# Six pairs of token-mixer projections as seven block products each, with operand sums on GpSimd

## What is computed

```python
h = rmsnorm(x, norm_mix) * (1.0 + sc1) + sh1            # sc, sh, g: 6 modulation rows, silu(cond) @ w_ada
proj = h @ w_in                                          # 1024 -> 7 groups of 512 columns
xr, gr, q_raw, ff, fb, iv, og = split(proj)
y_lru = rmsnorm(h_f + h_b, norm_lru) * gelu(gr)          # two RG-LRU scans over xr
y_hg  = hgrn2(q_raw, ff, fb, iv, og, ...)                # 4 heads, forward and backward, states 128x128
x = x + g1 * (concat([y_lru, y_hg]) @ w_out)
h = rmsnorm(x, norm_ffn) * (1.0 + sc2) + sh2
x = x + g2 * expert_choice_ffn(h, ...)                   # 16 SwiGLU experts, capacity 2T/16
y = rmsnorm(x, norm_final)
```

## Time and profile before

| | us |
|---|---|
| median of 3 runs (lowest, highest) | 958.57 (958.35, 960.14) |
| the profiled execution | 958.34 |
| its span, first to last instruction | 956.6 |
| PE busy | 928.8 (97%) |
| VectorE busy | 516.9 (54%) |
| ScalarE busy | 289.7 (30%) |
| GpSimd busy | 101.2 (11%) |

### The profile page before, as it was taken

How to read it: one execution, slowest core, us unless ns; L and a number is a source line. 1 busy time by engine, 2 the same in 40 slices (tenths; PEclk the granted TensorE clock), 3 DMA queues, 4 the chain that set the end, 5 groups by cost and what they waited for, 6 DMA issues and landing times.

```text
span 956.6 us, 19027 instructions
## 1 busy us (share of the span) xinstructions
PE 928.8 (97%) x8298; PEld 423.3 (44%) x8298; DVE 516.9 (54%) x1269; ACT 289.7 (30%) x507; POOL 101.2 (11%) x115
## 2 busy tenths in 40 slices
PE   5999999999999999999999999999999999999996
PEld 4555756768667554463222222222222223333332
DVE  4487667663654743764464461752636516444096
ACT  5137756564653824323020100200202002010103
POOL 3200010000000022112102002011020110100100
PEclk9999999999999999999999999999999999999999
DMA  9991014404029443168999999999999999999993
GB/s 333 334 386 52 2 55 157 160 5 176 10 92 367 174 164 150 66 240 323 403 399 404 408 416 408 415 401 413 418 405 413 405 413 425 401 426 413 412 380 122
DMA packets 52930, 276.15 MB, mean 289 GB/s; under 512 B 4400, under 2 KB 12752, under 8 KB 39920
## 3 DMA queue, kind: packets, MB, share of 16 engines
q1 hardware_dynamic: 45744, 253.77, 66.1%
q0 software_dynamic: 5584, 15.89, 5.7%
q10 hardware_dynamic: 1520, 5.28, 1.4%
HBM read 261.91 MB, written 13.01 MB: 287 GB/s over the span
## 4 chain that ended last, share of the span: by engine, by line
PE 79%; DMA 8%; DVE 5%; ACT 3%; issue 3%; POOL 0%; SPq 0%; POOLq 0%; DVEq 0%; ACTq 0%
PE pa L699 44%; PE p L699 34%; DMA ring<-in_w_up_dram 3%; DMA reg_e<-in_w_up_dram 3%; DMA ring<-in_w_ada_dram 1%; ACT reg_c L1374 1%; ACT L1374 1%; ACT reg_d L1374 1%; DMA reg_c<-h_rows,row_s 0%; ACT reg_b L1374 0%; DVE reg_a L2246 0%; DVE reg_b L1867 0%; PE p L854 0%; DVE reg_a L2241 0%; DVE reg_b L1838 0%
## 5 line engine op out<-in xcount | busy, mean ns | idle before, releaser
L699 PE MATMUL pa<-ring,reg_b 128*32 128x512 f32 (+1 forms) x1696 | 250.0, 593 | 0.7 <-DMA ring<-in_w_up_dram 0.5
L699 PE MATMUL p<-ring,reg_b 128*16 128x512 f32 (+1 forms) x1920 | 215.3, 592 | 1.1 <-issue 1.1
L699 PE MATMUL pa<-reg_a,ring 128*128 128x512 f32 (+1 forms) x640 | 191.2, 453 | 2.2 <-DVE reg_a L1730 1.5
L699 PEld LDWEIGHTS pa<-ring,reg_b 128*32 128x32 f32 (+1 forms) x1696 | 82.5, 117 | 143.7 <-issue 142.6
L699 PEld LDWEIGHTS pa<-reg_a,ring 128*128 128x128 f32 x640 | 98.3, 191 | 80.1 <-issue 79.9
L699 PEld LDWEIGHTS p<-ring,reg_b 128*16 128x16 f32 (+1 forms) x1920 | 63.9, 102 | 143.9 <-issue 143.9
L2142 DVE STREAM_TRANSPOSE reg_b<-reg_b 32x128 f32<-32x128 f32 x384 | 116.3, 303 | 5.9
L2158 DVE TENSOR_TENSOR reg_b<-reg_b,pa 128x512 f32<-128x512 f32 x16 | 11.0, 686 | 146.7 <-PE pa L699 146.4
L1374 ACT ACTIVATE reg_b<-pa 128x512 f32<-128x512 f32 (+1 forms) x20 | 12.4, 619 | 239.8 <-PE pa L699 239.8
L1374 ACT ACTIVATE reg_b<-reg_d,x_mod 128x128 f32<-128x128 f32 (+1 forms) x112 | 39.4, 440 | 140.7 <-PE p L699 140.7
L1374 ACT ACT_TABLE_LOAD x57 | 73.1, 1283 | 4.6 <-issue 2.8
(11 more groups left out here) (335 smaller groups left out, 937.4 us busy)
## 6 DMA issues: line engine op xcount, KB each, us to landing
ring<-in_w_gate_dram SPq DMA_DIRECT2D x25, 2048.0 KB, 21.1
ring<-in_w_down_dram SPq DMA_DIRECT2D x24, 2048.0 KB, 24.1
ring<-in_w_up_dram SPq DMA_DIRECT2D x22, 2048.0 KB, 21.5
ring<-in_w_ada_dram SPq DMA_DIRECT2D x8, 2048.0 KB, 8.5
ring<-in_w_in_dram SPq DMA_DIRECT2D x6, 2048.0 KB, 19.9
ring<-in_w_ada_dram SPq DMA_DIRECT2D x8, 1024.0 KB, 12.8
reg_a<-in_w_up_dram SPq DMA_DIRECT2D x4, 2048.0 KB, 20.3
reg_a<-in_w_gate_dram SPq DMA_DIRECT2D x3, 2048.0 KB, 18.1
```

The costliest lines, as they stand in the source:

```text
L699: return nc.tensor.matmul(out, lhsT, rhs, start=start, stop=stop, **kw)
```

## The change

Six pairs of projections, the first two items of units 0 to 5 (`TWOS`), are no longer computed item by item. The pair (one, two) is a 2x2 block matrix product: two token halves of 320, two halves of the input dimension, two blocks of 128 columns. It is made from seven block products (Strassen's scheme in Winograd's form) of four 128x320 matmuls each, 28 in place of 16 of 512 and 16 of 128 columns. Each product goes to a half of a `pa` tile (`banks`).

- GpSimd makes four sums of token blocks (128x1280 each, once, into slots 2 and 3 of the ring) and four sums of weight blocks per pair (128x512 each). The token sums and the weight sums of pairs 0 and 1 stand behind the hT_p copy; those of pair u+1 stand in unit u.
- ScalarE copies products 1 and 2 out of PSUM (`two_copy`, ahead of the exponentials), VectorE adds five products (`two_sum`, between its weighings), GpSimd makes two joins (`two_join`, 128x320). Silu for Q and OG follows at the end of units 0, 2 and 4.
- PE orders a unit anew: products 1 to 3, product 4, (head_norm,) products 5 and 6, turn_k, product 7. In unit 0 `ada_sum(4)` stands ahead of product 4 and `ada_sum(5)` behind product 6.
- `w_in`'s columns for the heads are loaded in 20 cells of 128 columns, in the order of use, by SyncE; slots 2 and 3 are thus free for the sums. `EARLY` is V of head 1 in place of FF.
- `marks_done` and `which_done` become one semaphore; `a2[0]` moves within its region.

The core of the diff:

```diff
+            pool.wait_ge(freed[2], 1)
+            pool.wait_ge(freed[3], 1)
+            nc.gpsimd.tensor_tensor(x_sum[0], x_quarter[1][0], x_quarter[1][1], ALU.add).then_inc(mixed, 1)
+            nc.gpsimd.tensor_tensor(x_sum[2], x_quarter[0][0], x_quarter[1][0], ALU.subtract).then_inc(mixed, 1)
+            pool.wait_ge(mixed, 2)
+            nc.gpsimd.tensor_tensor(x_sum[1], x_sum[0], x_quarter[0][0], ALU.subtract).then_inc(mixed, 1)
+            pool.wait_ge(mixed, 3)
+            nc.gpsimd.tensor_tensor(x_sum[3], x_quarter[0][1], x_sum[1], ALU.subtract).then_inc(mixed, 1)
+
+            def weight_sums(i):
...
+                if i >= 2:
+                    pool.wait_ge(two_ps, 7 * (i - 1))
+                t1, t2, t4 = w_sum[i % 2]
+                a, b = w_cell(one), w_cell(two)
+                nc.gpsimd.tensor_tensor(t1, b[:, 0:4, :], a[:, 0:4, :], ALU.subtract).then_inc(mixed, 1)
+                pool.wait_ge(mixed, weights_by(i) + 1)
+                nc.gpsimd.tensor_tensor(b[:, 0:4, :], b[:, 4:8, :], b[:, 0:4, :], ALU.subtract).then_inc(mixed, 1)
+                nc.gpsimd.tensor_tensor(t2, b[:, 4:8, :], t1, ALU.subtract).then_inc(mixed, 1)
+                pool.wait_ge(mixed, weights_by(i) + 3)
+                nc.gpsimd.tensor_tensor(t4, a[:, 4:8, :], t2, ALU.subtract).then_inc(mixed, 1)
...
+            weight_sums(0)
+            weight_sums(1)
             for u in range(2 * HEADS):
...
+                if 1 <= u < len(TWOS) - 1:
+                    weight_sums(u + 1)
+                if u < len(TWOS):
+                    two_join(u)
...
+            def product(i, bank, w, x):
+                for k in range(4):
+                    r = mm(banks[bank], w[:, k, :], x[:, k, :], k == 0, k == 3)
+                r.then_inc(two_ps, 1)
...
+            def two_middle(i):
+
+                one, two = TWOS[i]
+                pe.wait_ge(empty[1], USE[one] // 2)
+                pe.wait_ge(mixed, weights_by(i) + 4)
+                product(i, 2, w_sum[i % 2][0], x_sum[0])
+                product(i, 1, w_cell(one)[:, 4:8, :], x_quarter[0][1])
...
+            def two_third(i):
+
+                pe.wait_ge(two_cp, copied_by(i) + 2)
+                product(i, 2, w_cell(TWOS[i][1])[:, 4:8, :], x_sum[3])
+                product(i, 0, w_cell(TWOS[i][1])[:, 0:4, :], x_sum[2])
+
+            def two_last(i):
+
+                pe.wait_ge(two_add, 5 * i + 1)
+                product(i, 3, w_sum[i % 2][2], x_quarter[1][1])
+                pe.sem_inc(full, 2)
...
-            project_sample(FILL[0][0], range(0, 2))
+            two_start(0)
             lru_sum()
 
...
+            def unit_projections(u):
+                if u > 0:
+                    two_start(u)
+                if u == 1 or u == 3 or u == 5:
+                    pe.wait_ge(sc_done, NSC * u)
+                    ada_sum(ADA_UNIT[u])
+                two_middle(u)
                 if u == 0:
                     pe.wait_ge(ln_log, 1)
...
+                    ada_sum(ADA_UNIT[u])
+                two_second(u)
+                if u == 2 or u == 4:
+                    head_norm(u // 2 - 1)
+                two_third(u)
+                if u == 2 or u == 4:
+                    turn_k(u)
+                    two_last(u)
+                    return
+                if u <= 1:
+                    ada_sum(ADA_UNIT[u] + 1)
+                    turn_k(u)
+                    two_last(u)
+                else:
+                    two_last(u)
+                    ada_sum(ADA_UNIT[u] + 1)
+                    project_sample(FILL[u][2])
+                    turn_k(u)
+                    project_prompt(FILL[u][2])
+                ada_turn(ADA_UNIT[u])
...
+            def two_copy(i, step):
+                (one_a, one_b), (two_a, two_b) = two_out(TWOS[i][0]), two_out(TWOS[i][1])
+                act.wait_ge(two_ps, 7 * i + 1 + step)
+                A((one_a, two_b)[step], banks[2 * step], ACT.Copy).then_inc(two_cp, 1)
...
+            def two_sum(i, step):
+                (one_a, one_b), (two_a, two_b) = two_out(TWOS[i][0]), two_out(TWOS[i][1])
+                after, dst, src, bank = ((4, two_a, one_a, 3), (3, one_a, one_a, 1), (6, one_b, two_a, 0),
+                                         (5, two_a, two_a, 2), (7, one_b, one_b, 3))[step]
+                dve.wait_ge(two_ps, 7 * i + after)
...
+                V.tensor_tensor(dst, src, banks[bank], ALU.add).then_inc(two_add, 1)
...
+                if u < len(TWOS):
+                    two_sum(u, 0)
                 dve.wait_ge(exp_done, 6 * u + 1)
                 weigh(W[6], kk, om).then_inc(w6_done, 1)
+                if u < len(TWOS):
+                    two_sum(u, 1)
+                    two_sum(u, 2)
```

More of the change, by code:

```diff
@@ L17 @@
 T = TS + TP
+HALF = T // 2
 NT = T // P
@@ L468, in _, with cell_load, whole_load @@
             mixed(3)
-            for what, s in LOADS[1 + MIXED:]:
-                kind, i = what
-                turn = SLOT_OF[what][1]
-                if turn:
-                    sp_eng.wait_ge(freed[s], turn)
+            def cell_load(g, h):
+                src = w_in_v[:, :, g * 512 + h * P:g * 512 + (h + 1) * P]
+                sp_eng.dma_start(w_cell((g, h)), src).then_inc(loaded[CELL_BY[(g, h)][0]], 16)
+            def whole_load(kind, i):
+                s, turn = SLOT_OF[(kind, i)]
+                sp_eng.wait_ge(freed[s], turn)
                 src = {"ada": w_ada_v, "in": w_in_v, "out": w_out_v}[kind][:, :, i * 512:(i + 1) * 512]
                 sp_eng.dma_start(ring[:, s], src).then_inc(loaded[s], 16)
+            for g in (IN_Q, IN_OG, IN_FF, IN_FB):
+                cell_load(g, 0)
+            sp_eng.wait_ge(freed[0], 1)
+            cell_load(IN_V, 0)
+            cell_load(IN_Q, 1)
+            cell_load(IN_OG, 1)
+            cell_load(IN_V, 1)
+            sp_eng.wait_ge(freed[1], 1)
+            cell_load(IN_FF, 1)
+            cell_load(IN_FB, 1)
+            cell_load(IN_Q, 2)
+            cell_load(IN_OG, 2)
+            whole_load("ada", 4)
+            sp_eng.wait_ge(full, 3)
+            cell_load(IN_FF, 2)
+            sp_eng.wait_ge(full, 4)
+            cell_load(IN_FB, 2)
+            sp_eng.wait_ge(full, 5)
+            cell_load(IN_V, 2)
+            sp_eng.wait_ge(full, 6)
+            cell_load(IN_V, 3)
+            whole_load("ada", 5)
+            whole_load("ada", 6)
+            sp_eng.wait_ge(two_ps, 7)
+            sp_eng.wait_ge(*cells_by((IN_V, 3)))
+            cell_load(IN_Q, 3)
+            cell_load(IN_OG, 3)
+            whole_load("ada", 7)
+            sp_eng.wait_ge(two_ps, 14)
+            sp_eng.wait_ge(*cells_by((IN_OG, 3)))
+            cell_load(IN_FF, 3)
+            cell_load(IN_FB, 3)
+            for c in range(8, 12):
+                whole_load("ada", c)
+            whole_load("in", IN_GR)
+            whole_load("out", 0)
+            whole_load("out", 1)
             def expert_rows(i, m, kh, e):
@@ L1081, in _ @@
                     r.then_inc(rb_ps, 1)
[L1082 to L1098 removed]
+                project_sample(two, range(0, KT - 3))
+                turn_k(u)
+                project_sample(two, range(KT - 3, KT))
+            for u in range(UNITS):
+                if u < len(TWOS):
+                    unit_projections(u)
+                else:
+                    gate_projections(u)
                 updates(u)
@@ L1549, in _ @@
                         act.wait_ge(empty[n % 2], n // 2 + 1)
+                    if h >= 1:
+                        act.wait_ge(*silu_of(h))
                 f = rw[d]
```

179 lines of the change are left out of this document (122 added, 57 removed).

## The result

The changed kernel takes 990.9 us (median of 6 runs, 988.3 to 993.3) against 958.7 us for the kernel before beside it (6 runs, 958.0 to 960.7): a ratio of 1.033, 95% interval 1.031 to 1.035. It is slower, as forecast, but by 32 us where 13 were forecast, and above the range. The profiled execution took 990.63 us, with a span of 988.8.

A forecast was written before the change was run, and what follows sets the result against it. TensorE, busy 97% of the span, was taken to bound the kernel. 958.3 us plus 21.8 lost in unit 0 minus 8.5 saved in later units gave 971.6 us (chance 0.54), range 961 to 983.

The forecast's parts named there:

- The sign: Whole kernel: slower than before by over 2 us, given 0.93; within that 0.03, faster 0.04.
- the largest term: Unit 0: PE stands 20.4 us waiting for GpSimd's sums; unit 0 ends 21.8 us later in all.
- The hold: Before two_middle(0): PE waits from 131.6 to 152.0 us for eight GpSimd sums queued behind the LRU state's store.
- The clock in unit 0: Behind PE's long wait in unit 0: PE comes back at 1.2 GHz, costing between nothing and 5 us, taken as 2.5.
- The rest of unit 0: From 152.0 us: products, modulation sums, 1.7 us more wait for chunk 5, updates, scores; unit 0 ends at 176.7 us.
- 320-column products: PE's block products: 0.54 us each, so a pair takes 15.1 us instead of 17.3, 2.2 us less per unit.
- The blocking of VectorE by GpSimd: Rival, units 0, 1, 2, 4: two-input operations of both engines take turns, 7.8 us more, 979.4 us; chance 0.25.
- The later units: Units 1 to 5: units 1, 3, 5 save 6.8 us, units 2 and 4 1.7 us, 8.5 us in all.
- have slack: Units 1, 3, 5: PE reaches the scores after their operands are done, so each saves 2.2 us, unit 1 0.2 more.
- later units save nothing: Rival, units after unit 0: additions and joins ahead of the scores take the saving, 980 us; chance 0.12.
- Edits at nothing: Weight loads in 512 KB cells, later output chunks and the shared semaphore of the marks cost no time.
- The rival with 320-column products at the price of 512: Rival, PE's block products: a pair would take 24 us and the whole 1,010 us; given no weight.

The follow-up runs named there:

- PE kept at work: Changed kernel plus 22 idle 128x512 products on PE ahead of unit 0's first wait for GpSimd's sums: 989.1 us, ratio 1.031.
- the runs with additions and memsets: Kernel before, with five GpSimd additions or thirteen GpSimd memsets of 128x1024 put ahead of the hT_p copy: 966.0 us with additions, 959.4 with memsets.
- light sums: Changed kernel with GpSimd's weight sums of units 2 to 5 cut to 2 columns and all joins to 8 columns: 983.6 us, ratio 1.025.
- all sums light: Changed kernel with every one of GpSimd's sums and joins cut to 2 or 8 columns a block: 969.7 us, ratio 1.010.
- early: Changed kernel with the LRU state's store and its lst_done wait moved behind the token sums and units 0 and 1's weight sums: 981.8 us, ratio 1.023.
- The pipelined kernel: Changed kernel with all sums on VectorE, waits reordered, next unit's first product ahead of the scores in units 0, 1, 2, 4: 952.6 us, ratio 0.992.

## Why the prediction was right and wrong

The sign, the place and the largest term were right; the size was wrong, because terms were missing and the saving of the later units did not come.

- **The hold.** Forecast 131.6 to 152.0 us; it ended at 152.81. The queue behind `lst_done`, eight operations that PE waits for, four waits among them: this step held, with 2.88 us for a token sum instead of 2.96. Four sums were slower beside VectorE (3.35, 3.34, 1.84, 1.73 us), 2.0 us together.
- **The clock in unit 0.** Taken as 2.5 us behind the hold; 3.0 by the rows. Right. What was not in the sum: four later falls, in units 0, 1, 2 and 5, behind waits of 1.4 to 2.8 us. The step priced only the long hold. In the runs where the waits went, so did the falls.
- **The rest of unit 0.** Forecast 24.7 us with the clock; 28.5 measured, and 23.1 with PE kept at work. The clock behind the hold cost 0.5 us more, the wait for chunk 5 was 2.5 us instead of 1.7, the wait for the bias (0.7) had been left out, and a fall of the clock behind the wait for chunk 5 (1.6) came on top.
- **320-column products.** 0.54 us each, exactly; 2.15 us for four. The saving of PE's own work is real: 2.2 us a unit.
- **The blocking of VectorE by GpSimd.** The rival, priced 7.8 us and given 0.25. It happens in full: 3.27 became 14.39 us, 1.69 became 5.66, the runs with additions and memsets show it by itself, and it costs 7 us in the units alone, where the rival had 4.3. The joins among the weighings were priced rightly (0.9 to 1.7 us; 1.3 to 1.5 measured); unit 5 and the falls of the clock were missing. Its price in unit 0 was misplaced: I let it delay PE's return by 3.5 us, but there VectorE waited, not GpSimd, and PE's return came 0.8 us late.
- **The later units.** Forecast 8.5 us saved; measured 6.7 lost, and this is the step that failed, by two terms of nearly equal size. The first is the blocking, which the forecast put at nothing and left to the rival: 6.6 us. The second is the sentence that units 1, 3 and 5 "have slack": 8.5 us. I had compared PE's arrival at the scores with the weighings and overlooked what else PE waits for. In units 0 and 1 the scores wait for the modulation's bias, which stands behind the last weighing, the last sum and the reach on VectorE (1.2 us in unit 1 with light sums, 2.5 as given). In unit 5 V's bank is freed only by that last sum (1.5 and 2.8 us), and `ada_sum` at the head of units 3 and 5 waits for the masks (1.1 us each; as given in unit 5 only). In unit 1 PE stood 1.9 us without a semaphore, and with light sums a fall of the clock followed (1.7). For units 2 and 4 the step held: the forecast had scores at 19.5 us, with light sums they came at 19.6, and the 21.0 of the changed kernel are GpSimd's joins. The rival "later units save nothing" (980 us) gives the right sum for the order alone, but not for its reason, additions ahead of the scores of every unit.
- **Edits at nothing.** The cells cost no wait that the runs show, but one thing stays open: in unit 1 PE stood 1.9 us in the middle of 64 equal products with no semaphore to wait for ("issue"). Seven of the eleven versions of the changed kernel have such a stop in unit 1, of 1.1 to 2.6 us. The loads do not explain it by themselves: the DMA engines' share was 0.95 to 1.20 in the stop of three versions, but 0.01 in that of the changed kernel, just behind a stretch at 0.97. Whether its instructions came late was not tried.
- **A sum that does not come out.** The rival with 320-column products at the price of 512 adds up, by the forecast's own terms, to 971.6 + 6 x (24 - 15.1) = 1,025 us and not to 1,010. It had no weight and nothing rests on it.

Of the 32 us, then: 14 by GpSimd's sums in unit 0 (all sums light against the unit's light), 7 by its work in the units, 9.5 that stay even without them. By PE's rows with all sums light these last are all lost by the end of unit 0 (167.27 us for 154.91), with the 6.6 us of queue behind the state's store as the largest part; units 1 to 5 neither save nor lose. The sum is 30.7, and the difference to 32.2 is the spread between sets of runs.

## What to carry to other kernels

When products are saved on the engine that bounds a kernel, list for each stage every wait of that engine and what stands ahead of the releasing instruction on its queue; a stage whose second chain is equally long gives little or nothing back until work of the next stage fills it. Put the added element-wise work where an engine already waits, and price a two-input operation on GpSimd by what it holds up on VectorE as well as by its own time. Here the same change with the sums on VectorE, the waits of the units put in another order and one product moved across the unit's border is 0.8% faster than the kernel before; as given it is 3.3% slower.

## What the runs showed of the hardware

- GpSimd and VectorE do not share the loss evenly: beside GpSimd's chain of sums VectorE's products went from 3.27 to 14.39 us for four, while GpSimd lost 2.0 us in 18.5. One-input work with per-partition scalars stood as well (0.34 to 2.91 us in the convolution, run `early`), and so did one-input copies there (0.99 to 2.90 us for two). Thirteen memsets on GpSimd left VectorE's four products at 3.27 us.
- VectorE adds 128x1280 in 1.49 us and GpSimd in 2.88; 128x512 in 0.69 and 1.26 us.
- TensorE's granted clock fell to the lower level (0.52 for some 3 us) behind waits of PE of 2.5 us, of 1.5 and 1.4 us close together, and of 2.8 us in the changed kernel, not only behind the long hold. A stop of 1.9 us in unit 1 was followed by a fall with light sums and by none in the changed kernel (granted clock 1.00 from 187.2 to 190.6). The pipelined kernel, without the long waits in units 2 to 5, kept 1.00 from 190 to 300 us.
- The tiny GpSimd operations of 8 columns took 0.20 us each, and 0.7 to 0.9 us beside VectorE's products.
